# Rows of the second tile by an indirect DMA, rows of seven odd pairs picked by a product on chip, nine weight blocks

## The chip, the cores and the metric

The kernel runs on one core of one Trainium2 chip. The metric is the device time of one execution in microseconds, the median of several runs. The profiler's times come from one further execution.

## The reference, cut to what matters

One layer of a decoder works on 576 tokens (512 of a prompt, 64 of eight samples) of 1024 numbers in float32: a mixer (pooling and a short convolution between two projections), a layer norm, a mixture of experts, a second layer norm. The mixture picks for each token one of four expert groups, then two of that group's eight experts, and adds their outputs, each weighted by a gate:

```python
g_top, g_idx = lax.top_k(g_prob, 1)
e_top, e_idx = lax.top_k(e_prob, TOP_K_IN_GROUP)
for e in range(N_EXPERTS):            # 32 experts, w1, w3: 1024 x 512, w2: 512 x 1024
    hdn = jax.nn.silu(xf @ w1[e]) * (xf @ w3[e])
    acc = acc + combine[:, e:e + 1] * (hdn @ w2[e])
x = _layer_norm(DEEPNORM_ALPHA * x + f, ln2_g, ln2_b)
```

Every expert is used by some token, so all 96 weight matrices (2 MB each, 201 MB together) have to come from HBM.

## The kernel before, in words

**Mixer and routing.** In the first 190 us TensorE computes the mixer, VectorE the first layer norm. The rows after that norm lie in `x_tok` (SBUF, five tiles of 128 tokens) and are also written to `x1_dram` in HBM. VectorE then works out each token's experts and its slot in them.

**Tiles.** An expert's tokens fill a tile of up to 64 slots. There are 33 tiles, 0 to 32: one for each expert, and a second one (tile 9) for the expert with the most tokens, which is moved to place 8 (`SHARED`) if its number is at least `EARLY`; tiles 8 and 9 share one load of weights. For tile t TensorE multiplies by w1, turns the hidden rows of tile t-1, multiplies by w3, and then multiplies tile t-1's hidden rows by w2 (`tile(t)`, `into_hidden`, `turn_hidden`, `down`). All products are float32; those of a tile have 64 rows, so two column halves of the array work side by side.

**Rows of a tile.** Tiles come in pairs: pair m is tiles 2m and 2m+1. GpSimd fetches the rows of pairs 1 to 16 from `x1_dram` with an indirect DMA of up to 128 rows of 4 KB (`fetch`, `rows_of`); a slot without a token has an index out of bounds and moves nothing. Even pairs land in `xe`, odd ones in `xe_odd`. TensorE turns a pair at the end of an odd tile (`turn_pair`), ScalarE keeps the turned rows (`keep_xeT`) and starts the outputs with them (`fill`). Tiles 0 and 1 need no fetch: `fetch_first(i)` picks their rows with ten float32 products of a 0/1 matrix (`hot_first`) and `x_tok`. Between the two stands `token_table`, 20 small products whose result VectorE makes into the slots' gates and the indices of all later DMAs.

**Weights.** SyncE (SP) issues the loads in one list, `LOADS`: load 0 and 1 are w1 and w3 of tile 0; from tile 1 on come w1 and w3 of tile t and w2 of tile t-1. So load 9 is w3 of tile 3, load 11 w1 of tile 4, load 23 w1 of tile 8, load 26 w2 of tile 8, load 27 w1 of tile 10, load 32 w1 of tile 12, load 95 the last. There are nine blocks of 2 MB (`EARLY_BLOCKS`) and a tenth in the memory of `x_tok`, free once `fetch_first(1)` is done. Before a load, SP waits until the block's last use is over (`block_free`): loads 9 and 10 wait for loads 0 and 1 to be used, load 11 goes into the tenth block, and from load 12 on load n waits for the use of load n-10. A block shared by tiles 8 and 9 is free after tile 9. Waits are in order: a load behind a waiting one waits too. Loads up to expert `EARLY` - 1 have fixed addresses, later ones wait for `order_ready`.

**Outputs.** GpSimd stores a token's first expert output by indirect DMA (`store`), fetches it again when the second is there (`load`), and sends the normed rows (`send`).

Of the kernel before, what the change touches and what calls it, by code (L numbers as in the profile page):

```python
# [13 lines left out]
P = 128  # L14
# [6 lines left out]
NT = 5  # L21
# [31 lines left out]
BX, BXT = (3, 6), (4, 7)  # L53
BASE = 16512
# [5 lines left out]
EARLY = 4  # L60
# [15 lines left out]
PLACE = {load: n for n, load in enumerate(LOADS)}  # L76


def homes():


    block, before = [], []
    for n in range(len(LOADS)):
        old = None if n < EARLY_BLOCKS or n == 11 else n - EARLY_BLOCKS if n < 11 else n - EARLY_BLOCKS - 1
        before.append(old)
        block.append(n if n < EARLY_BLOCKS else EARLY_BLOCKS if old is None else block[old])
    return block, before


HOME, BEFORE = homes()  # L90
LANDED = [16 * HOME[:n + 1].count(b) for n, b in enumerate(HOME)]

# [11 lines left out]
def build(nc, x_prompt, x_sample, state_pool, state_conv, w_in, w_pool_map, pool_scale, conv_w, w_out,  # L104
# [3 lines left out]
    with ctx:  # L108
# [16 lines left out]
        tenth = at("tenth_block", X_AT, BLK)  # L125
# [18 lines left out]
        hot_first = at("hot_first", HOT_AT, 2, NT, SLOTS)  # L144
        silu = at("silu", HOT_AT + 4 * NT * PAIR, FH)[:, :]
# [21 lines left out]
        pair_row = nc.alloc_sbuf_tensor_at("pair_row", [P, PAIRS + 1], I32, offset=equal_at + 224)  # L167
        row_idx = [nc.alloc_sbuf_tensor_at(f"row_idx{j}", [P, 2], I32, offset=equal_at + 320 + 32 * j) for j in range(2)]
# [29 lines left out]
        def block_at(b):  # L198
            return tenth[:, :] if b == EARLY_BLOCKS else blocks[:, b, :]
# [11 lines left out]
        w_router = ye_flat[:, DP:DP + KD * NR].rearrange("p (k c) -> p k c", k=KD)  # L211
        b_router = ye_flat[:, DP + KD * NR:DP + KD * NR + NR]
# [68 lines left out]
        over = io_flat[:, 2688:2688 + XTILES * E].rearrange("p (a e) -> p a e", a=XTILES)  # L281
# [41 lines left out]
        table_done, table_ready = sem("table_done"), sem("table_ready")  # L323
        extra_ready, order_ready = sem("extra_ready"), sem("order_ready")
        block_loaded = [sem(f"block_loaded{b}") for b in range(EARLY_BLOCKS + 1)]
# [41 lines left out]
        def _(sp):  # L367
# [30 lines left out]
            def load_in(b, w, e):  # L398

                src = w[e] if isinstance(e, int) else w[bass.DynSlice(e, 1)].rearrange("e d f -> (e d) f")  # L400
                if isinstance(e, int) and e < 2:
# [74 lines left out]
            for n in range(EARLY_BLOCKS, EARLY_BLOCKS + 2):  # L476
                block_free(n)
                load(n)
# [1180 lines left out]
```

## Time and profile before

| | us |
|---|---|
| median of 3 runs (lowest, highest) | 708.28 (706.73, 708.86) |
| the profiled execution's own time | 707.71 |
| its span, first to last instruction | 706.0 |
| TensorE busy | 600.4 (85%) |
| VectorE, ScalarE, GpSimd busy | 306.9, 217.7, 160.9 |
| bytes by DMA | 235.99 MB, mean 334 GB/s |

The span is shorter than the execution's time by what lies ahead of the first and behind the last instruction. PE is TensorE, PEld its weight loads, DVE VectorE, ACT ScalarE, POOL GpSimd, SP SyncE; SPq is SP's queue of DMA issues. A busy TensorE need not be at its peak, since ends of products are modelled. L405 is line 405 of the kernel.

### The profile page before, as it was taken

The numbers are of one execution on the slowest core, as the hardware profiler recorded it, in microseconds if no ns is written. First come the engines' busy times: TensorE is split into PE (matmuls) and PEld (weight loads), VectorE is DVE, ScalarE is ACT, GpSimd is POOL, SyncE is SP. The second block draws the span as 40 slices with busy tenths as digits, with TensorE's granted clock in tenths as the row PEclk, the third lists the DMA queues.
The fourth block names the chain that finished last, engine by engine and source line by source line (L and its number), as shares of the span: only waits on it lengthen the run. The fifth ranks groups of instructions, "written<-read, shape, count | busy, mean of one in ns | idle before, by whom it ended". The sixth has DMA issues, their size and how long they took to land.

```text
span 706.0 us, 10591 instructions
## 1 busy us (share of the span) xinstructions
PE 600.4 (85%) x4200; PEld 413.1 (59%) x4200; DVE 306.9 (43%) x785; ACT 217.7 (31%) x315; POOL 160.9 (23%) x184
## 2 busy tenths in 40 slices
PE   6999999999999999999977777776777788787782
PEld 5999999878865655555534444443444444454350
DVE  4562485417576025444444333333333443333563
ACT  4232313302220224453433242414323242414130
POOL 1000000000000324334324223322223323232242
PEclk9999999999989999999999999999999999999997
DMA  9953033834497999999999999999999999999990
GB/s 263 285 178 130 7 121 119 355 124 180 158 393 264 340 420 418 417 413 423 421 414 420 412 421 418 421 422 421 422 421 418 418 418 420 419 422 415 419 378 25
DMA packets 45899, 235.99 MB, mean 334 GB/s; under 512 B 13576, under 2 KB 18184, under 8 KB 28745
## 3 DMA queue, kind: packets, MB, share of 16 engines
q1 hardware_dynamic: 32447, 220.92, 77.7%
q0 software_dynamic: 12544, 11.71, 4.9%
q10 hardware_dynamic: 857, 2.67, 1.0%
q8 instruction: 34, 0.56, 0.3%
q14 instruction: 17, 0.13, 0.0%
HBM read 237.69 MB, written 30.20 MB: 379 GB/s over the span
## 4 chain that ended last, share of the span: by engine, by line
PE 43%; SPq 39%; DMA 6%; DVE 6%; issue 3%; ACT 1%; POOL 0%; POOLq 0%; DVEq 0%; ACTq 0%
SPq L405 27%; PE ps L554 14%; SPq L409 12%; PE ps L719 11%; PE ps L611 7%; DMA blocks<-in_w 6%; PE ps L740 6%; SPq L429 1%; PE ps L640 1%; PE ps L632 1%; PE ps L517 1%; PE ps L705 1%; PE ps L624 1%; PE ps L728 1%; DMA x_tok<-in_x_prompt 1%
## 5 line engine op out<-in xcount | busy, mean ns | idle before, releaser
L719 PE MATMUL ps<-blocks,ln 128*64 128x256 f32 x1888 | 217.3, 383 | 46.5 <-DMA blocks<-in_w 45.0
L719 PEld LDWEIGHTS ps<-blocks,ln 128*64 128x64 f32 x1888 | 147.7, 138 | 118.3 <-issue 68.6
L740 PE MATMUL ps<-blocks,hT 128*64 128x512 f32 x496 | 113.4, 597 | 26.0 <-DMA blocks<-in_w 24.8
L740 PEld LDWEIGHTS ps<-blocks,hT 128*64 128x64 f32 x496 | 33.6, 136 | 87.0 <-issue 53.9
L1004 ACT ACTIVATE std<-rstd,eps 128x1 f32<-128x1 f32 x32 | 9.4, 295 | 212.7 <-DVEq L1544 212.7
L1512 DVE SCALAR_TENSOR_TENSOR h_rows<-silu,slot_gate,ps 128x256 f32<-128x256 f32 x33 | 15.9, 481 | 109.2 <-PE ps L719 109.1
L1110 POOL DMA_INDIRECT out<-prev,final_row x32 | 32.1, 1004 | 83.9 <-DVE prev L1550 83.0
L1106 POOL DMA_INDIRECT prev<-first_outputs,final_row x32 | 33.7, 1054 | 73.4 <-DMA first_outputs<-ye,first_row 41.7
L962 ACT ACT_TABLE_LOAD x30 | 38.5, 1283 | 24.0 <-PE ps L719 23.6
L821 ACT ACTIVATE ln<-ps 128x512 f32<-128x512 f32 (+1 forms) x38 | 19.9, 572 | 75.0 <-PE ps L705 54.1
L554 PE MATMUL ps<-xT_high,w_in_high 128*128 128x288 f32 x256 | 40.5, 300 | 2.8 <-ACT w_in_high L821 1.6
L1523 DVE TENSOR_TENSOR ye<-ye,ps 128x512 f32<-128x512 f32 x16 | 11.0, 688 | 68.3 <-PE ps L740 68.3
L1523 DVE TENSOR_TENSOR ye_more<-ye_more,ps 128x512 f32<-128x512 f32 x16 | 11.0, 688 | 67.9 <-PE ps L740 67.9
L554 PE MATMUL ps<-xT_low,w_in_high 128*128 128x288 f32 x256 | 39.1, 294 | 0.0
L554 PE MATMUL ps<-xT_high,w_in_low 128*128 128x288 f32 x256 | 39.1, 294 | 0.0
L1004 ACT ACT_TABLE_LOAD x30 | 38.5, 1283 | 0.6
L554 PEld LDWEIGHTS ps<-xT_high,w_in_high 128*128 128x128 f32 x256 | 35.8, 188 | 3.8 <-ACT w_in_high L821 2.0
L554 PEld LDWEIGHTS ps<-xT_low,w_in_high 128*128 128x128 f32 x256 | 35.7, 188 | 0.0
L554 PEld LDWEIGHTS ps<-xT_high,w_in_low 128*128 128x128 f32 x256 | 35.7, 188 | 0.0
L1102 POOL DMA_INDIRECT first_outputs<-ye,first_row x16 | 18.1, 1130 | 75.3 <-DVE ye L1523 74.1
L1102 POOL DMA_INDIRECT first_outputs<-ye_more,first_row x16 | 18.9, 1181 | 67.6 <-DVE ye_more L1523 66.4
L719 PE MATMUL ps<-tenth_block,ln 128*64 128x256 f32 x224 | 27.4, 399 | 7.6 <-DMA tenth_block<-in_w 7.6
(235 smaller groups left out, 786.6 us busy)
## 6 DMA issues: line engine op xcount, KB each, us to landing
blocks<-in_w SPq DMA_DIRECT2D x85, 2048.0 KB, 43.7
tenth_block<-in_w SPq DMA_DIRECT2D x9, 2048.0 KB, 44.3
blocks<-in_w_in SPq DMA_DIRECT2D x3, 2048.0 KB, 10.9
blocks<-in_w_out SPq DMA_DIRECT2D x2, 2048.0 KB, 7.8
blocks<-in_w SPq DMA_DIRECT2D x4, 1024.0 KB, 37.7
x_tok<-in_x_prompt SPq DMA_DIRECT2D x4, 512.0 KB, 5.1
blocks<-in_w_in SPq DMA_DIRECT2D x4, 512.0 KB, 10.9
first_outputs<-in_x_prompt SPq DMA_DIRECT2D x4, 512.0 KB, 8.7
```

The costliest lines, as they stand in the source:

```text
L405: sp.dma_start(in_block(b), src.rearrange("(p c) f -> p c f", c=KD)).then_inc(block_loaded[b], 16)
L409: sp.dma_start(out_block(b).rearrange("p (g c) d -> p g c d", g=2), src.rearrange("(g p c) d -> p g c d", g=2, c=KF // 2)).then_inc(block_ ...
L554: mm = pe.matmul(ps[:, 2 * (c % 2) + h, 0:HALF], w_part[a][:, c % 2, k, :], xT[b][:, k, h * HALF:(h + 1) * HALF], start=(i == 0 and k == 0 ...
L611: mm = pe.matmul(ps[0:r, o % 4, :], mix_part[a][:, k, j * P:j * P + r], wout_part[h][b][:, k, :], start=(i == 0 and k == 0), stop=(i == 2 ...
L719: mm = pe.matmul(ps[64 * g:64 * g + 64, bank, 0:FH], x, w[:, k, g * FH:(g + 1) * FH], start=(k == 0), stop=(k == KD - 1))
L740: mm = pe.matmul(ps[64 * g:64 * g + 64, BY, :], hT[:, k % 2, k // 2 * SLOTS:(k // 2 + 1) * SLOTS], w[:, k, g * DH:(g + 1) * DH], start=(k ...
L962: nc.scalar.activation(silu, ps[:, B1, 0:FH], ACT.Silu).then_inc(silu_ready, 1)
L1004: nc.scalar.activation(std[:, :], rstd[:, 1, 1:2], ACT.Sqrt, bias=eps[:, 1:2]).then_inc(std_ready, 1)
L1102: return g.indirect_dma_start(out=first_rows[:, :], out_offset=rows_at(idx), in_=ye[u], in_offset=None, bounds_check=last_row, oob_is_err= ...
L1106: return g.indirect_dma_start(out=prev[w], out_offset=None, in_=first_rows[:, :], in_offset=rows_at(idx), bounds_check=last_row, oob_is_er ...
L1110: return g.indirect_dma_start(out=prompt_rows[:, :], out_offset=rows_at(idx), in_=prev[w], in_offset=None, bounds_check=last_prompt_row, o ...
L1523: v.tensor_tensor(ye[u], ye[u], ps[:, BY, :], ALU.add).then_inc(y_kept, 1)
```

## The change

- **Nine blocks.** The tenth block is gone, and `x_tok` keeps the tokens' rows to the end. Load n waits for the use of load n-9, from load 9 on. Loads 9 to 13 have fixed addresses (`EARLY` is 5), so SP waits for `order_ready` and `table_ready` and loads `ln2` behind load 13.
- **Tile 1.** `fetch_first(1)` is gone. In the middle of `fetch_first` TensorE multiplies five times by one column of token numbers; ScalarE makes 64 indices of it; GpSimd fetches tile 1's rows with an indirect DMA into `xe`. `turn_second` turns them ahead of `token_table`. The order is then: w1 and w3 of tile 0, `turn_second`, `token_table`, w1 of tile 1, `turn_hidden(0)`, w3 of tile 1, w2 of tile 0.
- **Pairs 3, 5, ... 15** (`PICKED`) aren't fetched. At the end of tile 2m-2 TensorE picks pair m's 128 rows with ten float32 products of 128 x 128 by 128 x 512; VectorE makes their 0/1 matrix during tile 2m-3, ScalarE copies the two halves to `xe_odd`.
- **Pair 1** is fetched as soon as its indices are there, which VectorE now makes ahead of the gates.

```diff
-EARLY = 4
+EARLY = 5
...
+ORDERED = PLACE["w1", EARLY]
+HOME = [n % EARLY_BLOCKS for n in range(len(LOADS))]
+LANDED = [16 * (n // EARLY_BLOCKS + 1) for n in range(len(LOADS))]
+PICKED = list(range(3, PAIRS, 2))
...
-        tenth = at("tenth_block", X_AT, BLK)
...
             def block_free(n):
-                if BEFORE[n] is None:
-                    sp.wait_ge(fetched, 2)
-                    sp.wait_ge(x1_stored, 16 * NT)
-                    return
-                kind, t = LOADS[BEFORE[n]]
+                kind, t = LOADS[n - EARLY_BLOCKS]
...
+                for j in range(NT):
+                    if j == 2:
+                        pe.wait_ge(hot_ready, 2)
+                        for i in range(NT):
+                            mm = pe.matmul(ps[64:P, BY, 0:1], hot_first[:, 1, i, :], far_val[:, i:i + 1],
+                                           start=(i == 0), stop=(i == NT - 1))
+                        mm.then_inc(second_indexed, 1)
...
+            def turn_second():
+                pe.wait_ge(second_fetched, 16)
+                pe.wait_ge(xeT_ready, 1)
...
+            def pick_pair(m):
+                n = PICKED.index(m)
+                pe.wait_ge(hot_ready, n + 3)
+                wait(pe, xe_kept, 2 * n)
+                pe.wait_ge(y_filled, 1)
+                for g in range(2):
+                    for j in range(NT):
+                        mm = pe.matmul(ps[:, BX[g], :], hot[:, j, :], x_tok[:, j, g * DH:(g + 1) * DH],
+                                       start=(j == 0), stop=(j == NT - 1))
+                    mm.then_inc(fetched, 1)
...
-                token_table()
-                fetch_first(1, lambda: turn_hidden(0))
-                down(*place("w2", 0), 0, lambda: turn_first(1))
+                pe.wait_ge(table_rhs_ready, 1)
+                turn_second()
+                token_table()
                 pe.wait_ge(xeT_ready, 2)
                 into_hidden("w1", *place("w1", 1), 1, 1)
+                turn_hidden(0)
                 into_hidden("w3", *place("w3", 1), 1, 1)
+                down(*place("w2", 0), 0)
...
+                if t % 2 == 0 and (t + 2) // 2 in PICKED:
+                    pick_pair((t + 2) // 2)
...
+            def keep_xe(m):
+                act.wait_ge(xe_turned, 2 * m - 2)
+                for g in range(2):
+                    act.wait_ge(fetched, 2 * PICKED.index(m) + g + 2)
+                    copy(xe_of[1][:, g, :], ps[:, BX[g], :]).then_inc(xe_kept, 1)
...
+            pool.wait_ge(second_row_ready, 2)
+            pool.wait_ge(x1_stored, 16 * NT)
+            rows_of(xe, second_row[:, :]).then_inc(second_fetched, 16)
...
-                if t % 2 == 0 and t // 2 + 2 <= PAIRS:
+                if t % 2 == 0 and t // 2 + 2 <= PAIRS and t // 2 + 2 not in PICKED:
                     fetch(t // 2 + 2)
...
+            def make_hot(m):
+                dve.wait_ge(fetched, 2 * PICKED.index(m) + 1)
+                for i in range(2):
...
+                    last = v.tensor_tensor(hot[:, :, i * SLOTS:(i + 1) * SLOTS],
+                                           slots[:, :].unsqueeze(1).to_broadcast([P, NT, SLOTS]),
+                                           one.unsqueeze(2).to_broadcast([P, NT, SLOTS]), ALU.is_equal)
+                last.then_inc(hot_ready, 1)
```

## Rows read from the trace of the kernel before

**Rows 1.** The page: busy tenths in 40 slices of 17.65 us; chain's shares by engine.

```profile
PE   6999999999999999999977777776777788787782
DMA  9953033834497999999999999999999999999990
PE 43%; SPq 39%; DMA 6%; DVE 6%; issue 3%; ACT 1%; POOL 0%; POOLq 0%; DVEq 0%; ACTq 0%
```

**Rows 2.** Stretches: length, busy us of PE, PEld, DVE, ACT, POOL; clock, DMA share, GB/s.

```profile
210.00:214.00 4.00, 3.85 (x36) 2.63 (x38) 3.41 (x19) 1.51 (x3) 0.00 (x0) 1.00 0.05 20
214.00:226.00 12.00, 10.99 (x94) 6.07 (x90) 8.46 (x36) 0.45 (x2) 0.00 (x0) 1.00 0.89 351
226.00:230.00 4.00, 3.82 (x18) 1.61 (x20) 1.85 (x6) 1.05 (x3) 1.54 (x2) 1.00 0.57 172
222.00:242.00 20.00, 18.84 (x134) 10.04 (x132) 6.57 (x26) 5.91 (x11) 6.03 (x5) 1.00 0.83 313
250.00:300.00 50.00, 50.00 (x380) 27.89 (x376) 20.94 (x60) 19.20 (x26) 18.37 (x18) 1.00 1.01 417
342.00:500.00 158.00, 121.30 (x878) 71.31 (x876) 58.32 (x166) 51.65 (x70) 49.87 (x48) 1.00 1.01 419
500.00:674.00 174.00, 134.52 (x944) 80.23 (x940) 63.95 (x186) 56.01 (x77) 52.91 (x51) 0.98 1.01 420
```

**Rows 3.** SP's issues of loads 9, 10, 11, 12, in order of time.

```profile
213.86 0.34 SPq L405 DMA_DIRECT2D blocks<-in_w  x1
217.31 0.38 SPq L409 DMA_DIRECT2D blocks<-in_w  x1
226.81 0.36 SPq L405 DMA_DIRECT2D tenth_block<-in_w  x1
234.16 0.34 SPq L405 DMA_DIRECT2D blocks<-in_w  x1
```

**Rows 4.** PE: a turned pair; w1 of tiles 8, 9, 11; loads 33 and 40.

```profile
281.06 1.16 PE L705 MATMUL ps<-ident,xe_odd 128*128 128x128 f32 x8
...
308.72 3.62 PE L719 MATMUL ps<-blocks,ln 128*64 128x256 f32 x32
...
319.65 3.62 PE L719 MATMUL ps<-blocks,ln 128*64 128x256 f32 x32
...
342.74 3.62 PE L719 MATMUL ps<-blocks,ln 128*64 128x256 f32 x32
...
359.59 3.67 PE L719 MATMUL ps<-blocks,ln 128*64 128x256 f32 x32 [0.62 <-DMA blocks<-in_w]
...
397.17 3.23 PE L740 MATMUL ps<-blocks,hT 128*64 128x512 f32 x14 [1.58 <-DMA blocks<-in_w]
```

**Rows 5.** The page: DMA queue of GpSimd; packets, MB, share of 16 engines' span.

```profile
q0 software_dynamic: 12544, 11.71, 4.9%
```

**Rows 6.** The first tiles in order of time: start, us, engine, line.

```profile
203.44 4.51 PE L686 MATMUL ps<-x_tok,hot_first 128*64 128x512 f32 x20 [0.18 <-DVE hot_first L1429]
...
210.15 7.13 PE L719 MATMUL ps<-blocks,ln 128*64 128x256 f32 x64 [0.75 <-ACT ln L821]
...
217.56 0.42 DVE L1499 TENSOR_TENSOR io<-io,gates 128x255 f32<-128x255 f32 x1
...
218.03 2.84 PE L791 MATMUL ps<-io 128*64 128x153 f32 x40 [0.76 <-DVE io L1499]
...
239.39 3.67 PE L719 MATMUL ps<-blocks,ln 128*64 128x256 f32 x32 [0.73 <-ACT ln L821]
```

**Rows 7.** The page: ScalarE's group on one column; busy us, mean ns.

```profile
L1004 ACT ACTIVATE std<-rstd,eps 128x1 f32<-128x1 f32 x32 | 9.4, 295 | 212.7 <-DVEq L1544 212.7
```

**Rows 8.** Line 1124, the 16 fetches of pairs: issue to landing.

```profile
DMA to landing us min/median/max: 5.7/11.3/15.7
```

**Rows 9.** PE, in order of time: two float32 products over the full width, 288 columns each.

```profile
29.11 1.13 PE L566 MATMUL ps<-blocks,ye 128*128 128x288 f32 x4
```

**Rows 10.** Line 566 in 29 to 31 us: ns of one record, least, median, most.

```profile
L566 PE MATMUL ps<-blocks,ye x4: 405/406/406, 29.1 to 29.8; 128*128 128x288 f32 x4
```

More of the change, by code:

```diff
@@ L198, in block_at @@
         def block_at(b):
-            return tenth[:, :] if b == EARLY_BLOCKS else blocks[:, b, :]
+            return blocks[:, b, :]
         def in_block(b):
@@ L323, in build @@
         table_done, table_ready = sem("table_done"), sem("table_ready")
+        second_indexed, second_row_ready = sem("second_indexed"), sem("second_row_ready")
+        second_fetched, pairs_ready = sem("second_fetched"), sem("pairs_ready")
         extra_ready, order_ready = sem("extra_ready"), sem("order_ready")
-        block_loaded = [sem(f"block_loaded{b}") for b in range(EARLY_BLOCKS + 1)]
+        block_loaded = [sem(f"block_loaded{b}") for b in range(EARLY_BLOCKS)]
         hot_ready = sem("hot_ready")
@@ L400, in load_in @@
                 src = w[e] if isinstance(e, int) else w[bass.DynSlice(e, 1)].rearrange("e d f -> (e d) f")
[L401 removed]
+                if isinstance(e, int) and e == 0:
                     sp.dma_start(in_block(b).rearrange("p (g c) f -> p g c f", g=2),
@@ L474, in _ @@
             load(8)
-            for n in range(EARLY_BLOCKS, EARLY_BLOCKS + 2):
+            for n in range(EARLY_BLOCKS, ORDERED):
                 block_free(n)
@@ L479, in _ @@
             sp.wait_ge(order_ready, 1)
-            for n in range(EARLY_BLOCKS + 2, EARLY_BLOCKS + 4):
-                block_free(n)
-                load(n)
             sp.wait_ge(table_ready, 1)
@@ L487, in _ @@
                 sp.dma_start(ln2[64 * g:64 * g + 64, 1, :], ln2_b[half].partition_broadcast(SLOTS)).then_inc(ln2_loaded, 16)
-            for n in range(EARLY_BLOCKS + 4, len(LOADS)):
+            for n in range(ORDERED, len(LOADS)):
                 block_free(n)
@@ L744, in first_tiles @@
             def first_tiles():
-                fetch_first(0)
-                turn_first(0)
+                fetch_first()
+                turn_first()
                 pe.wait_ge(xeT_ready, 1)
@@ L1023, in _ @@
             for t in range(2, E):
+                if t % 2 and (t + 1) // 2 in PICKED:
+                    keep_xe((t + 1) // 2)
                 silu_of(t)
@@ L1577, in _ @@
             settled(v.scalar_tensor_tensor(far, slot_first[:, :], FAR, far, ALU.mult, ALU.add))
-            settled(v.tensor_scalar(none, line, 0.0, FAR, ALU.is_equal, ALU.mult))
-            settled(v.scalar_tensor_tensor(none, line, -1.0, none, ALU.add, ALU.add))
-            v.tensor_copy(token_row[:, :], none)
-            for i in range(2):
-                half = slice(64 * i, 64 * i + 64)
-                last = v.tensor_copy(pair_row[half, :], none[half, i:i + 2 * PAIRS + 1:2])
-            settled(last)
             settled(v.tensor_tensor(none, line, again, ALU.is_equal))
@@ L1609, in _ @@
                     final(t - 2)
+                if t % 2 and (t + 3) // 2 in PICKED:
+                    make_hot((t + 3) // 2)
             add_y((E - 2) % YR, E - 2)
```

101 lines of the change are left out of this document (63 added, 38 removed).

## The prediction, made before the change was run

> **What bounds the kernel now.** First the slices of the page [rows 1]: from the 15th on DMA stands at 9 in each, while PE falls to 7 and 8. The chain that ended last lies 39% on SP's queue, which waits for blocks to come free. The stretches [rows 2] say it sharper: from 342 to 674 us the DMA engines are busy 1.01 of the time at 419 to 420 GB/s, PE only 0.77 (121.30 of 158, 134.52 of 174). So from 250 us on the end is set by the bytes that the 16 engines still have to move. A microsecond of PE costs nothing there as long as loads keep queueing, and every microsecond in which the engines have nothing to do, early or late, is in the total. They have such gaps: a share of 0.05 from 210 to 214, 0.57 from 226 to 230, 0.83 over 222 to 242, or 3.4 us idle [rows 2]. These are the waits of loads 9, 11 and 12 for their blocks: issues at 213.86, 226.81, 234.16 [rows 3]. Later PE waits for landings: w3 of tile 12 (load 33) starts at 359.59, w2 of tile 13 (load 40) at 397.17 [rows 4], so one load takes 37.58 / 7 = 5.37 us, with all other traffic beside it.
>
> **Term 1, seven fetches go: -6.0 us.** Routing the reference's inputs gives the tiles' sizes: pairs 1 to 16 fetch 1114 rows of 4 KB, of these pairs 3, 5, ..., 15 fetch 538 (104, 43, 74, 101, 62, 69, 85), 2.20 MB. The profile agrees in sum: GpSimd's queue moved 11.71 MB [rows 5]; stores, loads and sends move each of 576 tokens' 4 KB once each, 7.08 MB, which leaves 4.63 MB for the fetches. The queue's packets took 4.9% of 16 engines' span, 34.6 us or 2.95 us per MB: 6.5 us for 2.20 MB. At the rate of the whole stream, 419 GB/s, it is 5.25 us. The rest of that queue moves rows of 2 KB, smaller than these; I take 6.0 and keep 5.2 and 6.5.
> The Trainium skill, page "DMA: Bandwidth & Descriptors", section "Anatomy of one DMA — SWDGE (gpsimd) path", prices the moving part of a DMA by its bytes over 436 GB/s. By that, an estimate, the seven fetches are 5.0 us, and the sum below would be 1.0 us smaller.
>
> **Term 2, the first tiles: -2.0 us.** What counts is when the engines run dry and when the next load is issued.
> (a) Five index products (10 records) come into fetch_first. The nearest row is the token table: 40 records with as wide a weight tile in 2.84 us, 0.07 each [rows 6], so 0.7; none at the least, twice as much if the weight loads overlap less. Tile 0's w1 starts at 210.85 instead of 210.15 [rows 6], and loads 9 and 10 are issued 0.7 later, at 214.6 and 218.0. The engines, idle by then, idle 0.7 longer.
> (b) Tile 1's fetch: its indices are ready about 203.44 + 1.8 (two of five row groups of 4.51) + 0.7 + 0.3 (ScalarE on one column [rows 7]) = 206.2. Fetches land 5.7 to 15.7 us after issue, median 11.3 [rows 8]: 211.9 to 221.9, median 217.5. It is needed when the token table's operands are ready: 217.98 [rows 6] and two small VectorE operations, 218.3. By the median no wait; at the longest 3.6 us, with the token table, the gates and all of tile 1 behind it. GpSimd has nothing else to do then.
> (c) turn_second, 8 transposes like a pair's 1.16 [rows 4], less their overlap: 1.1, to 219.4. token_table 2.84: to 222.3. ScalarE turns out the rows meanwhile. w1 of tile 1 takes 3.5: to 225.8, and load 11 is issued at 225.85. turn_hidden and w3 take 4.0, load 12 at 230.0; w2 of tile 0 3.5, load 13 at 233.5 (together 10.9, the period of tile 8: 319.65 - 308.72 [rows 4]). What VectorE now does ahead of the gates (seven small operations) ends before the gates' user, turn_hidden, at 225.8. SP's waits for order and table are over by load 13; their cover gone, they would hold loads 14 on alone.
> (d) Before, load 11's bytes began to flow 0.9 us after its issue: 2.3 us of busy time in 226 to 230 [rows 2]. Loads 9 and 10 were drained at about 226 (351 GB/s x 12 us is two loads); now 0.7 later. Load 11 flows from 226.75, about when they end, and loads 12 and 13 queue behind without a gap. I put 0.7 + 0.3 + 0.4 for small gaps = 1.4 us idle against 3.4: 2.0 gained. An earlier tile 1 thus makes up for the tenth block. Bounds: 2.7 if (a) costs nothing; 3.6 + 0.7 less if (a) and (b) both go worst, a loss of 2.3.
> Tile 2 starts at 235.4 instead of 239.39 [rows 6]. Pair 1's fetch, issued about 224, could make that 4 later if it takes 15.7 us; the engines have loads 11 to 13 until 242.
>
> **Term 3, nine blocks and the picks: 0.** A pick is ten products of 128 x 512. Over the full width two products of 288 columns make four records and take 1.13 us with the last one's modelled 0.406 [rows 9, 10]: (1.13 - 0.406) / 3 = 0.24 a record, two records for a product, so 0.86 for 512 columns. A pick is 8.6 us, all seven 60. From 250 on that is PE time under a DMA bound: four tiles take PE about 46 us, with a pick 55, the DMA 12 x 5.3 = 64. ScalarE's two copies and VectorE's 0/1 matrix (two comparisons, four small operations, some 2 us) stand beside other tiles' products on engines busy for less than half of the span.
> The place to check is the pair of tiles that shares its blocks, where none comes free for long. Tile 8's w1 starts at 308.72 now [rows 4]; then at 308.72 - 4.0 + 8.6 (pair 3's pick) = 313.3, when load 31 is issued. Load 32 waits for w1 of tile 9: a tile (10.9), pair 5's pick (8.6), a w1 (3.5): 336.3; it flows from 337.2. The engines: before, load 31 landed about 359.6 - 2 x 5.37 = 348.9, less up to 1.8 us from last byte to product; the new kernel is ahead by 2.0 (term 2) and by 147 rows of pairs 3 and 5 (1.6), so they run out between 343.5 and 345.3. Some 7 us are left. Loads 32 to 34 last 16.1 us, to 360; load 35 waits for w2 of tile 9, 19.6 us after load 32 (342.74 - 319.65 - 3.5 [rows 4]): it flows at 356.8, 3 us in time. Elsewhere up to eight loads stand behind the block in use. I take 0 and keep up to 5 us of idle, for this margin is thin.
>
> **Sum.** -6.0 - 2.0 + 0 = -8.0 us on the profiled execution's 707.71 (span 706.0): 699.7. That execution is 0.57 under the median of the runs, 708.28, so 700.3.
>
> **Rivals.**
> A, slower: the picks run at half clock. Place: tiles 8 and 9. A pick of 17.1 us moves load 32 to 354.2 (two picks, 8.5 each), 9.7 us behind the engines' last byte, and load 35 leaves 3.5 us idle; with terms 1 and 2 that is +5.2: 713.5. It decides from a pick of about 15 us on. Against it: the granted clock is 1.00 and 0.98 (the 2.4 GHz level) from 250 to 674, although from 342 on PE waited for most loads [rows 2, 4].
> The Trainium skill, page "TensorE: Matmul & The Clock Gate", section "HAM oscillation — how this bites in real kernels", says that PE work cut up by waits for DMA falls back to half rate; it is the rule that would bring A about, and this trace doesn't show it.
> B, much of the gain is eaten at the same place, because PE runs some microseconds later than I have it (a pick of 11 us, or a late tile 2): 2 to 6 us of idle, 702.3 to 706.3, say 704.3. For it: the margin of 3 us is a difference of long sums.
> C, more gain: fetches disturb the loads beyond their bytes, as a second queue on the same engines, and term 1 is 10 us: 696.3. Against: the shares are 1.01 with and without them.
> D, the removal doesn't do what it says: loads go at a pace of their own and the freed time isn't used, 707. Against: the engines' GB/s holds at 417 to 420 whatever mix they move [rows 2].
>
> **How the numbers follow.** Forecast 0.64, B 0.16, C 0.07, A 0.07, D 0.06. A measurement here can tell about 0.3% (2.1 us) from no change, so faster is below 706.2, slower above 710.4: forecast, C and most of B give faster 0.85, D and the rest of B same 0.08, A slower 0.07. The forecast's own range, from its bounds, is 698 to 703.5; to hold 8 in 10 it takes in half of B and of C: 697 to 705.
>
> **What would show it.** Term 1: GpSimd's queue falls to about 9.6 MB. Term 2: load 11 issued near 226, 12 near 230, 13 near 233.5; DMA share over 222 to 242 above 0.93. Term 3: products of 0.86 us; a share of 1.0 from 330 to 365; PE busy for about 0.9 from 400 on. It is wrong if a slice behind the 15th shows DMA below 9, if load 32 is issued behind 344, or if tile 1's fetch holds turn_second past 219.

## The result, and the profile after

| | before | after |
|---|---|---|
| median (lowest, highest), us | 708.52 (706.73, 712.80), 12 runs | 704.76 (699.54, 707.22), 12 runs |
| profiled execution, us | 707.71 | 701.69 |
| its span, us | 706.0 | 699.9 |
| TensorE busy, us | 600.4 (85%) | 650.9 (93%) |

The ratio over all runs is 0.9939, with the 95% interval 0.9911 to 0.9966 (the two medians alone give 0.9947). Two more series of the same kernel, on two chips, gave 0.9908 [0.9879, 0.9938] and 0.9932 [0.9905, 0.9959]. The change makes the kernel faster, by less than one percent: by 3.8 to 6.1 us at the medians of the three series and by 6.0 us between the two profiled executions; 8.0 was forecast. One later run of the kernel before, 1016.49 us at a granted clock of 0.558, is left out of the ratios as a slow one.

The page of the changed kernel, against [rows 1, 5]: the slices of TensorE and DMA, GpSimd's queue, the chain that ended last by engine, and the weights' loads from issue to landing, with that line of the kernel before behind it.

```profile
PE   5999999999998999999999999999998899799782
DMA  9861231835297999999999999999999999999991
q0 software_dynamic: 11680, 9.58, 4.2%
PE 66%; DMA 23%; DVE 6%; issue 2%; SPq 1%; ACT 1%; POOL 0%; POOLq 0%; DVEq 0%; ACTq 0%
blocks<-in_w SPq DMA_DIRECT2D x94, 2048.0 KB, 27.6
...
blocks<-in_w SPq DMA_DIRECT2D x85, 2048.0 KB, 43.7
```

TensorE, at 6 to 8 from the 21st slice on before, stands at 9 up to the 30th and falls to 7 to 9 behind it, and the chain now runs through it for 66%, no longer through SP's queue (1% in place of 39%). A load landed 27.6 us after its issue in the median, 43.7 before. That looks like a kernel bound by TensorE, but the DMA digits haven't moved: the bytes still set the end, with TensorE close behind. How close is the point of several experiments.

Stretches of the changed kernel, columns as in [rows 2]:

```profile
210.00:214.00 4.00, 2.57 (x21) 1.76 (x22) 3.52 (x16) 2.54 (x4) 0.00 (x0) 1.00 0.72 298
214.00:226.00 12.00, 11.66 (x124) 8.65 (x120) 7.46 (x30) 1.04 (x3) 1.25 (x2) 1.00 0.75 295
222.00:242.00 20.00, 18.73 (x160) 11.52 (x158) 8.30 (x31) 6.17 (x10) 5.79 (x5) 1.00 0.99 387
356.00:362.00 6.00, 6.00 (x46) 2.97 (x42) 2.88 (x9) 0.18 (x1) 2.25 (x2) 1.00 0.84 293
342.00:500.00 158.00, 157.68 (x1035) 83.43 (x1030) 70.22 (x209) 63.30 (x87) 51.98 (x50) 1.00 1.01 414
500.00:670.00 170.00, 150.17 (x998) 82.94 (x998) 64.37 (x189) 59.42 (x82) 48.64 (x47) 1.00 1.01 420
```

Over 222 to 242 us the DMA share is 0.99 and was 0.83: 0.2 us idle in place of 3.4. The dry stretch ahead of load 9 is still there, a little later. A new one has come, 356 to 362: a share of 0.84 is 1.0 us idle. From 500 us on the rate is the 420 GB/s of before. TensorE is busy for all but 0.3 of the 158 us from 342 to 500.

The first tiles of the changed kernel, TensorE's work in order of time, against [rows 6]:

```profile
205.00 1.94 PE L677 MATMUL ps<-x_tok,hot_first 128*64 128x512 f32 x8 [0.22 <-DVE hot_first L1473]
...
212.28 7.13 PE L734 MATMUL ps<-blocks,ln 128*64 128x256 f32 x64 [0.75 <-ACT ln L840]
219.75 1.16 PE L695 MATMUL ps<-ident,ln 128*128 128x128 f32 x8 [0.34 <-DVE io L1545]
220.84 2.84 PE L810 MATMUL ps<-io 128*64 128x153 f32 x40
223.51 3.62 PE L734 MATMUL ps<-blocks,ln 128*64 128x256 f32 x32
...
237.01 3.24 PE L734 MATMUL ps<-blocks,ln 128*64 128x256 f32 x28 [0.73 <-ACT ln L840]
```

Tile 1's fetch, and its time from issue to landing:

```profile
L1164 POOL DMA_INDIRECT ln<-x_rows,second_row x1: 1207/1207/1207, 208.0 to 208.0; - x1
...
DMA to landing us min/median/max: 6.9/6.9/6.9
```

`turn_second` (L695), at 219.75, waits 0.34 us for VectorE's table operands, not for tile 1's rows: they had landed at about 215.

SP's issues in the changed kernel: loads 9, 10, then 11 and 12 in one row, 13, against [rows 3]; further on loads 31, 32 and 33 in one row, 34, and 35 with the next.

```profile
216.00 0.34 SPq L402 DMA_DIRECT2D blocks<-in_w  x1
219.45 0.38 SPq L406 DMA_DIRECT2D blocks<-in_w  x1
227.17 4.37 SPq L402 DMA_DIRECT2D blocks<-in_w  x2
234.65 0.38 SPq L406 DMA_DIRECT2D blocks<-in_w  x1
...
315.63 0.38 SPq L406 DMA_DIRECT2D blocks<-in_w  x1
339.80 3.66 SPq L402 DMA_DIRECT2D blocks<-in_w  x2
343.55 0.38 SPq L406 DMA_DIRECT2D blocks<-in_w  x1
359.44 0.81 SPq L402 DMA_DIRECT2D blocks<-in_w  x2
```

TensorE at the shared pair, w1 of tile 8, pair 5's pick, w1 of tile 9:

```profile
315.42 3.62 PE L734 MATMUL ps<-blocks,ln 128*64 128x256 f32 x32
...
326.59 8.85 PE L706 MATMUL ps<-x_tok,hot 128*128 128x512 f32 x20
335.37 3.68 PE L734 MATMUL ps<-blocks,ln 128*64 128x256 f32 x32
```

A pick takes 8.85 us, and load 35 is issued only at 359.44, behind w2 of tile 9: that is the new dry spot.

### The profile page after: what moved, and what is told of

Its sections match the earlier page's. It is cut to its first block, busy times and chain, and to the rows that moved or that the text cites. A ratio compares the mean times of both kernels' runs of the same rounds, so it can differ in the third digit from the quotient of the medians.

```text
span 699.9 us, 10915 instructions
## 1 busy us (share of the span) xinstructions
PE 650.9 (93%) x4334; PEld 427.5 (61%) x4334; DVE 316.4 (45%) x829; ACT 226.2 (32%) x330; POOL 155.1 (22%) x180
## 4 chain that ended last, share of the span: by engine, by line
PE 66%; DMA 23%; DVE 6%; issue 2%; SPq 1%; ACT 1%; POOL 0%; POOLq 0%; DVEq 0%; ACTq 0%
DMA blocks<-in_w 21%; PE ps L734 20%; PE ps L544 14%; PE ps L755 11%; PE ps L706 8%; PE ps L601 7%; PE ps L720 2%; DMA blocks<-in_w_in 1%; PE ps L743 1%; SPq L402 1%; PE ps L630 1%; PE ps L614 1%; DVE blocks L1307 1%; PE ps L556 0%; PE ps L810 0%
## 5 line engine op out<-in xcount | busy, mean ns | idle before, releaser
L734 PE MATMUL ps<-blocks,ln 128*64 128x256 f32 x2112 | 241.2, 381 | 16.3 <-DMA blocks<-in_w 14.8
L734 PEld LDWEIGHTS ps<-blocks,ln 128*64 128x64 f32 x2112 | 153.1, 137 | 102.8 <-issue 36.0
L755 PE MATMUL ps<-blocks,hT 128*64 128x512 f32 x528 | 120.2, 597 | 7.9 <-DMA blocks<-in_w 5.7
L755 PEld LDWEIGHTS ps<-blocks,hT 128*64 128x64 f32 x528 | 37.1, 137 | 69.9 <-issue 58.1
L706 PE MATMUL ps<-x_tok,hot 128*128 128x512 f32 x140 | 62.0, 598 | 0.0
L706 PEld LDWEIGHTS ps<-x_tok,hot 128*128 128x128 f32 x140 | 26.1, 190 | 35.7 <-issue 35.7
L1146 POOL DMA_INDIRECT prev<-first_outputs,final_row x32 | 34.0, 1061 | 61.2 <-DMA first_outputs<-ye,first_row 36.7
L1583 DVE COPY hT<-ps 128x256 f32<-128x256 f32 x33 | 13.9, 420 | 62.5 <-PE ps L743 62.5
## 6 DMA issues: line engine op xcount, KB each, us to landing
blocks<-in_w SPq DMA_DIRECT2D x94, 2048.0 KB, 27.6
```

The source lines that it names most:

```text
L706: mm = pe.matmul(ps[:, BX[g], :], hot[:, j, :], x_tok[:, j, g * DH:(g + 1) * DH], start=(j == 0), stop=(j == NT - 1))
L734: mm = pe.matmul(ps[64 * g:64 * g + 64, bank, 0:FH], x, w[:, k, g * FH:(g + 1) * FH], start=(k == 0), stop=(k == KD - 1))
L755: mm = pe.matmul(ps[64 * g:64 * g + 64, BY, :], hT[:, k % 2, k // 2 * SLOTS:(k // 2 + 1) * SLOTS], w[:, k, g * DH:(g + 1) * DH], start=(k ...
L1146: return g.indirect_dma_start(out=prev[w], out_offset=None, in_=first_rows[:, :], in_offset=rows_at(idx), bounds_check=last_row, oob_is_er ...
```

## The experiments

**How the traces are split.** Whole times differ by several microseconds between runs of one kernel, so each trace is cut in three: the front, up to the start of `hot_first` on VectorE (`202.89` in the kernel before); the middle, from there to the end of the last packet of 8 KB or more on SP's queue, the weights' last byte; and the tail, what is left of the span. In us:

| kernel | front | middle | tail | span |
|---|---|---|---|---|
| before | 202.9 | 487.9 | 15.2 | 706.0 |
| before_again | 202.7 | 488.1 | 15.2 | 706.0 |
| after | 204.5 | 480.5 | 14.9 | 699.9 |
| after_again | 203.2 | 480.3 | 18.0 | 701.5 |
| after_third | 203.7 | 479.7 | 14.8 | 698.2 |
| all_fetched | 204.2 | 485.4 | 15.2 | 704.8 |
| thin_picks | 205.0 | 479.7 | 14.8 | 699.5 |
| shared_late | 202.3 | 479.0 | 14.8 | 696.1 |
| shared_late_again | 205.1 | 480.9 | 18.5 | 704.5 |
| before_no_fetch | 203.6 | 482.7 | 14.4 | 700.7 |
| before_nine | 202.5 | 493.8 | 15.2 | 711.5 |
| double_picks | 207.1 | 495.0 | 42.4 | 744.5 |
| after_warm | 203.2 | 481.9 | 16.9 | 701.9 |
| shared_late_warm | 202.0 | 480.6 | 18.2 | 700.8 |

Where one kernel has several traces its middle varies by 0.2 (before), 0.8 (after) and 1.9 us (shared_late): differences under about 1 us are not read. All ratios are to the kernel before, run beside each.

**before_again** is the kernel before unaltered, the mark for what can be told apart.

> The kernel before once more, unaltered, for a second trace and the granted clock of each of its runs. In the traces so far the middle, from hot_first to the last byte of the weights, took 487.9 us before and 480.5 and 480.3 for the changed kernel, while what lies ahead of it (202.3 to 205.0) and behind it (14.8 to 18.0) varied with single stretches of 3.4 us at half clock there. Theory: the change is worth 7.5 us in the middle in every run, and the rest of the medians' difference is this scatter; then the middle of this trace is 487 to 489. Rival: the middle itself varies by some us from run to run.

Measured: 707.86 us (707.08 to 714.13, 12 runs), 1.0007 [0.9987, 1.0027]; the same span and the same three parts within 0.2 us; the middle of 488.1 is as expected.

**after_again** and **after_third** are the changed kernel unaltered, in later series.

> The changed kernel once more, unaltered, as the mark for the other runs of this call and for a second trace. Its first twelve times lay between 699.5 and 707.2 us and fell as the granted TensorE clock rose (0.978 to 0.990). Theory: this scatter comes from stretches at half clock in the first 205 us, where TensorE's chain is the bound, and not from the change; then two traces differ ahead of the first tile (hot_first at 204.46 us in the first trace) by as much as their spans do, and agree to 1 us from there to the end (495.4 us). Rival: the scatter arises behind 205 us, at the tiles that share a block, where the DMA engines ran dry by 1.8 us; then the part behind hot_first differs by several microseconds. Median expected 703 to 705.

Measured: 701.71 us (699.19 to 705.83, 6 runs) beside 707.77; middle 480.3, tail 18.0. The median is below the 703 to 705 expected, and the theory failed: the front is 1.3 us shorter than in the first trace while the span is 1.6 us longer. Nor is it the rival's place, the tiles that share a block: the middle agrees within 0.2 us, and the tail is 3.1 us longer.

> The changed kernel once more, as the mark for this series and for a third trace. Of the changed kernel two traces stand: 699.9 us with three half-clock stretches of TensorE (13.6, 197.9 and 693 us), and 701.5 us with five (11.4, 195.8, 663.4, 683.9 and 694 us); its unprofiled runs scatter from 699.2 to 707.2 us, 1.1%, where those of the kernel before keep mostly to 707 to 709 us. Theory S: the stretch from hot_first to the last byte of the weights is the same in every run (480.3 to 480.5 us in both traces), and the runs differ by what half-clock stretches cost ahead of hot_first and behind the last byte. It expects 480.0 to 481.0 us of that stretch in this trace too, a median of 699 to 706 us with the runs spread over 5 us and more, and a longer run wherever the run's mean granted clock is lower. Rival D: the dry spot of the DMA engines behind load 35 (up to 1.4 us) opens and closes from run to run and the middle scatters with it: 479 to 484 us.

Measured: 704.03 us (699.96 to 707.33, 7 runs) beside 709.13; middle 479.7, which is 0.3 under the range expected, tail 14.8. The runs follow the mean granted clock: 699.96 us at 0.990, 703.13 to 704.03 at 0.985 to 0.986, 704.46 and 704.77 at 0.984, 707.33 at 0.980. The kernel before, beside them, follows it less closely: 706.6 to 709.5 us at 0.982 to 0.991, 707.4 to 712.5 at 0.977 to 0.980.

**before_no_fetch: term 1 alone.** In the kernel before, the odd pairs from 3 on are not fetched, and tiles 6, 7, 10, 11, ... work on pair 1's rows.

```diff
-                pe.wait_ge(x_fetched[m % 2], 16 * ((m + 1) // 2))
+                pe.wait_ge(x_fetched[m % 2], 16 * ((m + 1) // 2) if m % 2 == 0 else 16)
...
-                if t % 2 == 0 and t // 2 + 2 <= PAIRS:
+                if t % 2 == 0 and t // 2 + 2 <= PAIRS and t // 2 % 2 == 0:
                     fetch(t // 2 + 2)
```

> The kernel before with the seven odd pairs from pair 3 on not fetched (their tiles use pair 1's rows, which stay in xe_odd); no pick, ten blocks, old first tiles. Theory, term 1 alone: 5.2 to 6.5 us less in the middle than before, 481.4 to 482.7. Rival (more gain than bytes, because a second queue disturbs the loads): 8 to 10 us less. Rival (the loads keep a pace of their own): no change.

Measured: 702.30 us (700.84 to 703.93, 6 runs), 0.9917 [0.9902, 0.9933]; middle 482.7. GpSimd's queue on its page:

```profile
q0 software_dynamic: 11536, 9.50, 4.1%
```

2.21 MB less than [rows 5], as the routing says, and the middle is 5.2 to 5.4 us shorter: term 1 by itself. 2.21 MB in 5.3 us is 417 GB/s, the rate of the whole stream; the queue's packets took 28.9 us of 16 engines in place of 34.6. So rival C (10 us) and rival D (nothing) are both out.

**all_fetched: the change without the picks.** Nine blocks, tile 1 by indirect DMA, but all pairs fetched as before.

```diff
-PICKED = list(range(3, PAIRS, 2))
+PICKED = []
```

> The seven odd pairs are fetched by DMA again, no picks; nine blocks, the kept tokens' rows and the new first tiles stay. Theory: term 1 (5.2 to 6.5 us of DMA) is lost again and the dry stretch of 1.8 us with it: 3.4 to 4.7 us above the changed kernel and 2 to 3 below the kernel before (first tiles alone, -2.0 forecast). Rival: the tenth block was worth something in the long stretch; then it is slower than the kernel before.

Measured: 706.53 us (704.53 to 709.29, 12 runs), 0.9979 [0.9961, 0.9996]; middle 485.4, that is 2.6 us under before: term 2. The medians show less of it than expected, 1.2 us under the kernel before in place of 2 to 3, and 4.8 above after_again. Its stretch of 222 to 242 us:

```profile
222.00:242.00 20.00, 19.27 (x164) 11.79 (x162) 8.31 (x31) 6.16 (x10) 5.79 (x5) 1.00 0.98 385
```

From here to the changed kernel the middle falls by 4.9 to 5.7 us, so in this order the seven fetches are worth what they were in the old one, and the picks that replace them cost nothing that can be told. The rival, a tenth block that is worth something in the long stretch, doesn't show: from 342 to 670 us the DMA share is 1.01 here and in before_nine, as in the kernel before [rows 2].

**before_nine: the tenth block alone.** The kernel before, in its old order, with nine blocks.

```diff
-        old = None if n < EARLY_BLOCKS or n == 11 else n - EARLY_BLOCKS if n < 11 else n - EARLY_BLOCKS - 1
+        old = None if n < EARLY_BLOCKS else n - EARLY_BLOCKS
...
-        block.append(n if n < EARLY_BLOCKS else EARLY_BLOCKS if old is None else block[old])
+        block.append(n if old is None else block[old])
...
-                if BEFORE[n] is None:
-                    sp.wait_ge(fetched, 2)
-                    sp.wait_ge(x1_stored, 16 * NT)
-                    return
```

> The kernel before without its tenth block: load n waits for the use of load n-9; first tiles and fetches as before. Load 11 then waits for w1 of tile 1 (done at 234.1) instead of 226.8, load 12 for w3. The engines are drained at 226.2 and idle until about 235: some 9 us instead of the 3.4 before, so the middle is 5 to 6 us longer, 493 to 494, and the time about 713. Rival, a block more or less is hidden: within 1 us of the kernel before. Rival, nine blocks also starve the long stretch: more than 8 us slower, with DMA shares below 0.98 behind 250 us.

Measured: 714.99 us (713.22 to 716.18, 4 runs), 1.0102 [1.0085, 1.0120]; middle 493.8, 5.8 us longer, both as expected within 2 us. Its stretch of 222 to 242 us:

```profile
222.00:242.00 20.00, 18.83 (x136) 10.19 (x134) 6.25 (x25) 6.05 (x11) 6.01 (x5) 1.00 0.53 197
```

The engines idle 9.4 us of these 20, 6.0 more than before [rows 2]. So tile 1's earlier place is worth 5.8 + 2.6 = 8.4 us, most of which pays for the lost block.

**thin_picks: picks of 1.98 us.** Only the first of five row groups is multiplied, so tokens of the other groups get no row.

```diff
-                    for j in range(NT):
+                    for j in range(1):
...
-                                       start=(j == 0), stop=(j == NT - 1))
+                                       start=(j == 0), stop=True)
```

> Of the five row groups of each pick only the first is multiplied (four fifths of the picked rows' sum are left out), so a pick takes about 1.8 us of TensorE instead of 8.85; nothing else changes. Theory: the picks cost time only where the DMA engines run dry for lack of a free block, 1.8 us near 360 us; expected 1.5 to 2.5 us below the changed kernel, and no drop of the DMA share between 345 and 365. Rival 1, TensorE is a bound of its own up to 500 us (busy 157.7 of 158 there): 5 us or more below. Rival 2, the picks are wholly hidden: within 0.7 us of it.

Measured: 704.12 us (699.91 to 707.25, 12 runs), 0.9951 [0.9931, 0.9971]; middle 479.7. Pair 5's pick, and the stretch of 356 to 362 us, which has no dry spot:

```profile
319.69 1.98 PE L706 MATMUL ps<-x_tok,hot 128*128 128x512 f32 x4
...
356.00:362.00 6.00, 6.00 (x50) 3.53 (x48) 4.27 (x14) 1.86 (x4) 2.05 (x2) 1.00 1.03 419
```

48 us less of TensorE's work (seven times 6.87) shorten the middle by 0.0 to 0.8 us, and the median is 2.4 us above after_again's of the same series, not 1.5 to 2.5 below; its runs show clocks of 0.969 to 0.990, after_again's 0.985 to 0.989. Under the DMA bound the picks are free, but for that dry spot.

**double_picks: picks of 17.4 us, rival A.** Every product of a pick is done twice.

```diff
-                    for j in range(NT):
+                    for j in [*range(NT), *range(NT)]:
```

> The changed kernel with every pick multiplied twice over (same result), 17.5 us of TensorE at full clock: the price of the prediction's rival A without its cause. By the prediction's sum for it: 13 us of idle engines near tiles 8 to 10 (changed kernel: 1 to 2) and four tiles that need TensorE for as long as DMA, so the middle 10 to 14 us longer than the changed kernel's 480.4, 491 to 495, and slower than the kernel before by about 4. Rival, picks are hidden: within 2 us of the changed kernel. Rival, TensorE becomes the bound for the whole stretch: over 500.

Measured: 744.72 us (741.08 to 746.21, 5 runs), 1.0504 [1.0480, 1.0529]; middle 495.0, at the upper end of what was expected. Pair 3's pick, and two stretches:

```profile
273.56 17.43 PE L706 MATMUL ps<-x_tok,hot 128*128 128x512 f32 x40
...
345.00:361.00 16.00, 16.00 (x77) 8.02 (x78) 0.42 (x1) 2.86 (x4) 1.45 (x2) 1.00 0.12 30
500.00:670.00 170.00, 170.00 (x1010) 87.76 (x1006) 65.32 (x195) 58.20 (x80) 51.97 (x50) 1.00 1.01 419
```

And TensorE's last products, w1 and w3 of tile 32, then its w2:

```profile
715.14 7.11 PE L734 MATMUL ps<-blocks,ln 128*64 128x256 f32 x64
...
726.08 6.38 PE L755 MATMUL ps<-blocks,hT 128*64 128x512 f32 x16 [0.61 <-DVE hT L1583]
```

The dry spot came where rival A has it: 14 us of these 16, and the middle is 14.5 to 15.3 us longer than after's. But the kernel lost three times that. From 500 to 670 the loads run at 1.01 again, so DMA loses nothing more there; TensorE works all of these 170 us and doesn't catch up. When the weights' last byte lands (702.1) it has the products of the last two tiles still to do, and its last w2 starts 24 us later: the tail is 42.4 us. The end is set by TensorE's work here, no longer by the bytes.

**shared_late and shared_late_again: the shared pair put elsewhere.** Tiles 20 and 21, not 8 and 9, share a load of weights.

```diff
-SHARED = 8
+SHARED = 20
```

> One constant: the two tiles that share their weights are tiles 20 and 21 instead of 8 and 9, so the long time in which no block comes free falls where up to eight loads are queued. Same result. Theory: the 1.8 us of dry DMA engines near 360 us go, 1.5 to 2.5 us below the changed kernel, DMA share 1.0 or more from 250 us to the end. Rival: the dry spot only moves to 560 to 600 us, since TensorE still has 23 us without freeing a block there: same time. A share below 0.98 there would show it.

Measured: 701.39 us (697.89 to 705.85, 6 runs), 0.9917 [0.9885, 0.9949]; middle 479.0. The stretch of 356 to 362 us here, and in after_third:

```profile
356.00:362.00 6.00, 6.00 (x52) 3.67 (x50) 4.72 (x15) 1.68 (x3) 1.20 (x1) 1.00 1.05 439
...
356.00:362.00 6.00, 6.00 (x50) 3.39 (x46) 4.04 (x14) 1.02 (x2) 1.42 (x2) 1.00 0.94 335
```

The dry spot is gone; in after_third it is 0.4 us, in after 1.0.

> SHARED = 20 alone, beside the changed kernel on the same chip. If the dry spot behind load 35 is real (1.4 us in the changed kernel's middle, 479.0 us against 480.4 us): 1 to 2 us below after_third by the medians, middle 478.5 to 479.5 us. If it is only scatter of the first series: within 0.5 us of after_third, middle 480 to 481 us.

Measured: 702.21 us (699.47 to 707.30, 8 runs), 0.9905 [0.9872, 0.9939]; middle 480.9. The medians are 0.3 and 1.8 us under the changed kernel's of the same series, the middle is once 1.3 us under and once 1.2 us over. Part of the 1.2 us over has another cause. In shared_late_again the clock was at 0.50 from 205.9 to 209.3 us, in the products of `fetch_first`:

```profile
205.67 3.50 PE L677 MATMUL ps<-x_tok,hot_first 128*64 128x512 f32 x8 [0.22 <-DVE hot_first L1473]
```

These eight records take 1.94 us in the trace of after, and the engines idle 5.3 us in the first 20 us behind the start of `hot_first`, where shared_late has 4.1. Less these 1.2 us its middle is 479.7, an estimate, which is the least that the changed kernel has. In the old order such a fall cost less: in before_again `fetch_first` took 6.02 us in place of 4.51, and the middle is 0.2 us longer. Whether the dry spot's 0.4 to 1.0 us is worth anything is left open: it lies within what two traces of one kernel differ by.

**after_warm and shared_late_warm: what scatters.** Four products of `ident` by itself stand ahead of each block of tiles 30 and 31 and of w1 of tile 32, in the changed kernel and in shared_late.

```diff
+            def tail_warm(seq, last_too=False):
+                if isinstance(seq, int) and (30 <= seq < E or seq == E and last_too):
+                    for _ in range(4):
+                        pe.matmul(ps[:, BX[0], 0:P], ident[:, :], ident[:, :], start=True, stop=True)
...
+                tail_warm(seq, kind == "w1")
...
+                tail_warm(seq)
```

> Four products of ident with ident (about 0.28 us each, into a bank that nobody uses by then) ahead of each block of tiles 30 and 31 and of w1 of tile 32, at places where TensorE waits 0.4 to 2.7 us for a block's bytes in the trace of the changed kernel. Theory S: in after_again two half-clock stretches at 663.4 and 683.9 us cost 3.1 us behind the last byte; with TensorE busy there they don't come, the part behind the last byte is 14.8 to 15.2 us, and the slow end of the scatter goes (the runs keep within 4 us of each other, median 700 to 702 us); the stretches ahead of hot_first stay, so some of the scatter stays. Rival F: the scatter is made ahead of hot_first or in the middle alone: the runs spread over 6 us and more as without the edit, with the same median as after_third within 1 us. Rival W: the products come at the wrong place and stand in the way of the weights' products: 1 to 3 us slower than after_third.

Measured: 705.05 us (702.52 to 705.77, 6 runs), 0.9933 [0.9906, 0.9960]; middle 481.9, tail 16.9, where a median of 700 to 702 and a tail of 14.8 to 15.2 were expected.

> Tile 20 instead of 8 shares its pair with the extra tile's work (SHARED = 20), and the same products ahead of the last tiles' blocks: both edits that could still gain. The middle without the dry spot is 479.0 us as in shared_late (1.4 us less than the changed kernel), the part behind the last byte 14.8 to 15.2 us: a profiled span of 696 to 698 us and a median of 698 to 701 us, the best of the series, 1 to 3 us below after_third. If the half-clock stretches in the last tiles are not what scatters: the same as shared_late_again within 1 us. If the products stand in the way: 1 to 3 us above shared_late_again.

Measured: 702.15 us (700.90 to 702.60, 6 runs), 0.9891 [0.9867, 0.9916]; tail 18.2, where a median of 698 to 701 was expected.

To read these, the last two tiles of two traces side by side. TensorE in after_third (span 698.2): w3 of tile 31, w2 of tile 31, tile 32's hidden rows turned, w2 of tile 32.

```profile
662.52 3.67 PE L734 MATMUL ps<-blocks,ln 128*64 128x256 f32 x32 [2.72 <-DMA blocks<-in_w]
...
668.12 3.65 PE L755 MATMUL ps<-blocks,hT 128*64 128x512 f32 x16 [0.61 <-DVE hT L1583]
...
681.27 0.51 PE L743 MATMUL ps<-ident,h_rows 128*128 128x128 f32 x2 [0.67 <-DVE h_rows L1578]
682.56 3.65 PE L755 MATMUL ps<-blocks,hT 128*64 128x512 f32 x16 [0.78 <-DVE hT L1583]
```

The same of shared_late_again (span 704.5):

```profile
665.46 5.36 PE L734 MATMUL ps<-blocks,ln 128*64 128x256 f32 x32 [2.53 <-DMA blocks<-in_w]
...
672.75 3.65 PE L755 MATMUL ps<-blocks,hT 128*64 128x512 f32 x16 [0.61 <-DVE hT L1583]
...
685.83 0.51 PE L743 MATMUL ps<-ident,h_rows 128*128 128x128 f32 x2 [2.30 <-DVE h_rows L1578]
687.11 5.35 PE L755 MATMUL ps<-blocks,hT 128*64 128x512 f32 x16 [0.78 <-DVE hT L1583]
```

The products by w3 of tile 31 and w2 of tile 32 in after_again (span 701.5):

```profile
662.88 5.36 PE L734 MATMUL ps<-blocks,ln 128*64 128x256 f32 x32 [2.49 <-DMA blocks<-in_w]
...
684.54 4.99 PE L755 MATMUL ps<-blocks,hT 128*64 128x512 f32 x16 [0.78 <-DVE hT L1583]
```

Two stretches of shared_late_again, then two of the kernel before; the last three numbers are the granted clock, the DMA share and GB/s:

```profile
666.70:670.10 3.40, 3.40 (x20) 2.40 (x17) 0.57 (x1) 0.00 (x0) 1.99 (x2) 0.50 1.03 427
687.20:690.60 3.40, 3.40 (x10) 1.16 (x12) 0.69 (x1) 0.00 (x0) 2.14 (x2) 0.50 0.18 57
...
579.90:583.30 3.40, 3.40 (x20) 2.41 (x18) 2.33 (x9) 1.73 (x3) 0.50 (x1) 0.51 0.99 404
617.50:620.90 3.40, 3.40 (x18) 2.39 (x16) 0.00 (x0) 0.58 (x1) 1.10 (x2) 0.50 1.02 424
```

From the start of w3 of tile 31 to the span's end it is 35.7 us in after_third and 35.8 in after, but 39.0 in shared_late_again and 38.6 in after_again. In the two longer ones the clock was at 0.50, the 1.2 GHz level, during w3 of tile 31 (5.36 in place of 3.67 us) and during the last w2 (5.35 and 4.99 in place of 3.65): 3.4 and 3.0 us, which is the difference. Nothing catches it up, for this is a chain: once w2 of tile 31 is there, VectorE norms two tiles ahead of tile 32's `products`, and those hidden rows are turned 13.1 us after w2 of tile 31 began in both traces.

So Theory S is shown for the tail of two longer traces; of a run of 707 us there is no trace, and the rest of its length stays open. What it says of the middle, the same in every run, doesn't hold: the fall in `fetch_first` of shared_late_again stands in after_warm too (3.55 us in place of 1.94, and 5.4 us of idle engines in the first 20 us). The kernel before has stretches at that level as well (0.51 at 579.9 us, 0.50 at 617.5), but where TensorE had time to spare [rows 2]. The remedy failed: with the added products the longest runs are gone (nothing above 705.8, and above 702.6 with `SHARED` at 20), but so are the shortest, for the products stand in the chain: from the start of w3 of tile 31 to the end it is 36.5 us in the trace of after_warm, with no stretch at 0.50 before 695.1. The runs took 702.5 to 705.6 us at a clock of 0.988 to 0.990, where the changed kernel's runs at 0.989 and 0.990 took 699.5 to 701.7. This fits rival W, though by the medians after_warm is only 1.0 us above after_third, within both intervals; and in shared_late_warm the last w2 took 5.26 us all the same. That last kernel has the lowest ratio of all; six of after_third's seven runs are longer than its longest, yet the intervals overlap, so no version is shown to beat the change.

## Why the prediction was right, and where its sizes were off

The direction was right: 704.76 us lies in the range, near its upper end of 705, and 4.5 us above the point forecast. That it lies in the range is in part luck. The forecast's own range ended at 703.5; what reached up to 705 was added for rival B, of whose idle engines 0.4 to 1.0 us came in place of 2 to 6, and the rest of what lifts the median to near B's 704.3, the front, the tail and the scatter of the runs, is in no term. Nor does that range follow "from its bounds": taken together they give 699.1 (6.5 and 2.7 us gained) to 710.4 (5.2 gained, 2.3 lost, 5 idle). Terms 1 to 3 describe the middle. They said -8.0 us; the three traces of the changed kernel have 7.4 to 8.4 us less middle than the two of before, 7.8 in the mean. The sizes behind that sum, and what lies outside it, need the corrections.

**Term 1, forecast -6.0, measured -5.2 to -5.4** (before_no_fetch). The step that failed is the choice between the two bounds: I went between the queue's mean 2.95 us per MB [rows 5] and the stream's rate, but these fetches cost just the stream's rate, 417 GB/s. Rows of 4 KB are hardly dearer here than the weights, and the trace of before had that price: a packet of 4096 bytes of this queue took 162 ns there in the mean and 159 in the median, one of 8192 bytes of the weights' queue 319 in the mean. Over 16 engines, 538 of the first are 5.3 to 5.5 us. The queue's mean is raised by what else it moves, and not by rows of 2 KB alone, as I had it: beside the 538 there are 1662 packets of 4096 bytes, 1284 of 2052 and 9060 of 4 and 8 bytes, the last at 9 ns each or 5.3 of the 34.6 us. By the Trainium skill, page "DMA: Bandwidth & Descriptors", section "Anatomy of one DMA — SWDGE (gpsimd) path", the seven fetches were 5.0 us, an estimate; the run stands nearer to that than my 6.0. Rival C is out: nothing beyond the bytes came back.

**Term 2, forecast -2.0, measured -2.6** (all_fetched). Counted from the first product of `fetch_first` (203.44 before, 205.00 after) the steps were:

| step | forecast | measured |
|---|---|---|
| w1 of tile 0 | 7.4 | 7.3 |
| `turn_second` | 14.9 | 14.8 |
| load 11 issued | 22.4 | 22.2 |
| load 13 issued | 30.1 | 29.7 |
| w1 of tile 2 | 32.0 | 32.0 |

(b), the fetch's landing, had room to spare: 6.9 us where 11.3 was the median [rows 8]. It also moved less: the queue's packets of 4096 bytes are 2200 before and 2219 in all_fetched, so tile 1 fetched 19 rows, where a pair fetches 70 in the mean (1114 / 16). The mis-sized parts are the 0.7 that the first gap was to grow by and the 0.3 + 0.4 of (d). By the packets, the engines idle 3.9 to 4.1 us in the first 20 us behind the start of `hot_first`, 4.4 and 4.6 before, and in the next 20 us 0.0 to 0.3, 2.4 and 3.2 before. That tile 1's early place just outweighs the tenth block is what before_nine shows, by 8.4 against 5.8 us.

**Term 3, forecast 0 with up to 5 us of idle, measured 0.4 to 1.0 of idle.** The pick took 8.85 us in place of 8.6. Load 31 came 0.8 us later than forecast (from the same anchor), load 32 1.9, load 35 2.0, and load 35 was to be 3 us in time; the engines are idle 1.0 us there in the trace of after and 0.4 in after_third. Load 35 stands 19.64 us behind load 32, as forecast; most of its delay lies in the tile between, 24.2 us from load 31 to load 32 where 23.0 was worked out. The rest of the margin went on the other side: by the packets load 31 was through at about 343.4 us, where the forecast gives 345.1 to 346.9 from the same anchor. Rival B was the right mechanism with a price of 1 us at most, not 4.

**Rival A, 713.5 forecast for a pick of 17.1 us, 744.7 measured.** Its dry spot was right, the price wrong by 31 us. The step that failed: a pick was weighed only at tiles 8 and 9, and "that is PE time under a DMA bound" was taken to hold behind them. The whole budget decides. Doubling the picks adds 7 x 8.85 = 62 us of TensorE and makes the span 44.6 us longer than after's 699.9, so the change left 17 us of slack, or 20 if double_picks' longer front (2.6 us) is taken off: 2.5 to 2.9 per pick (after's own row has 19.8 us of idle TensorE from 500 to 670). The rows would have shown it: TensorE has idle slices only from the 21st on [rows 1], that is from 353 us, not from the 15th as I read them, and its idle time behind 342 us is 36.7 + 39.5 = 76 us [rows 2], and the picks take 62 of it. By that estimate A decides from a pick of 11 to 12 us, not 15. For the same reason "PE busy for about 0.9 from 400 on" failed: 1.00 up to 500 and 0.88 behind, as TensorE first works off the blocks that filled while it was late.

**From the middle to the median.** Between the traces the change is worth 6.1 us (706.0 against 699.9, the mean of three), not 7.8. 0.7 of the rest is the tail, 3.1 us longer in one trace of three, by the lower clock. 1.0 is the front, 203.8 in the mean against 202.8. All kernels with the new front lie at 202.0 to 205.1 (207.1 in double_picks), those with the old one at 202.5 to 203.6; whether the change did that or chance is open. It touches that part too, by an edit that the list of the change leaves out: w1 and w3 of expert 1 are loaded in rows of 16 KB in place of 8 (`load_in`). So the step that took the whole -8.0 us off "the profiled execution's 707.71" assumed wrongly that what lies ahead and behind stays as it was. The medians give as much or less (6.1, 5.1, 3.8 us), as many runs are the longer ones at a lower clock; what lengthens the longest of them, no trace shows.

The rule cited beside rival A (the Trainium skill, page "TensorE: Matmul & The Clock Gate", section "HAM oscillation — how this bites in real kernels") says that TensorE's work cut up by waits for DMA falls back to half rate. That has its cases here, but not where A needs it: the level fell in w3 of tile 31 behind a wait of 2.5 us for a load, and again behind one of 2.30 us for VectorE, never during the picks (no record of L706 took over 0.70 us in after). In after_third, with a wait of 2.72 us ahead of the same w3, it didn't fall; what makes the difference is open. That "this trace doesn't show it", as I wrote there, is not quite so: the 0.98 of [rows 2] comes from the two falls at 579.9 and 617.5 us, behind waits of 1.95 and 2.02 us for loads.

## What to carry to other kernels

Under a DMA bound, weigh added work on another engine against its idle time over the whole stretch and not only at the tightest spot: 62 us on TensorE were free, 124 us cost 45. Price bytes taken off a saturated stream at the stream's rate, unless a run shows more. Where several runs of a kernel scatter, cut each trace at two fixed events; here the part that the change is about agrees within 1 us between traces of one of the two kernels, where the runs' times differ by 7. Look at the granted clock inside that part too before a difference is read.

## What was not expected of the hardware

- The granted clock fell to 0.50 in the last tiles of some executions and not of others of the same kernel, at a cost of 3.0 to 3.4 us; the same falls in the kernel before cost nothing, as loads set the pace there.
- Tile 1's fetch, 64 indices of which 19 rows were moved, issued ahead of load 9, landed in 6.9 us; the pairs' fetches in the full stream took up to 15.7 us before [rows 8] and 12.9 after.
- A float32 product of 128 x 512 over the full width took 0.885 us in the row of ten, near the 0.86 scaled from 288 columns [rows 9, 10].
